# State-space groups: the gated y moves into the upper squares tiles, and GpSimd takes two steps of the group's tail

## The chip, the cores and the metric

The kernel runs on one core of one Trainium2 chip. The core has a matrix engine (TensorE; PE in the profile, its weight loads PEld), VectorE (DVE), ScalarE (ACT), GpSimd (POOL) and SyncE (SP), which here only issues DMAs. The metric is device time in microseconds of one execution. The kernel before took 1147.05 us, the median of 3 runs from 1146.51 to 1148.46.

## The reference

A sequence of 256 tokens of width 1024 goes through three layers in float32: sparse attention with a convolved feed-forward layer, retention with another, and a hybrid layer. The change lies in the hybrid layer's state-space branch:

```python
y = ssd_chunked_scan(x32 * dt[..., None], dt * a_cont, bmat, cmat)
y = y + d_skip.astype(jnp.float32)[:, None] * x32
y = y.reshape(b, seq, D_INNER).astype(h.dtype) * jax.nn.silu(z)
y = rmsnorm(y.reshape(b, seq, SSD_GROUPS, D_INNER // SSD_GROUPS),
            ssd_norm_w.reshape(SSD_GROUPS, D_INNER // SSD_GROUPS))
y_ssd = y.reshape(b, seq, D_INNER) @ w_branch_ssd
```

There are four groups of 512 channels. In each, y is gated by silu(z) and normalised over the 512 channels of its group. Beside this branch run a pooling branch and two gates; their products are merged afterwards.

## The kernel before

Every matrix product is computed in three passes of a reduced format: a weight is split into a high part (ScalarE, `split_hi`, line 235) and a low part (VectorE, `split_lo`, line 240: raw minus high), and so is each operand. Weights come as 512 KB slabs of 128 x 1024 through a ring of six; TensorE works a slab in 24 matmuls (lines 248 to 250), some 2.7 us.

In the state-space stage each engine has its own program in a fixed order, tied to the others by semaphores. A group has 12 slabs, j = 0 to 11. Slabs 0 to 5 are B, C and four tiles of x: ScalarE evicts the slab with the first tap of the convolution (line 1840), VectorE adds the three others (line 2009, which read PSUM), ScalarE applies silu (line 1789). At j = 6 TensorE turns x (`turn`, lines 1660 and 1663, which wait for the last silu). Slabs 6 to 9 are z, 10 and 11 are the pooling input. From j = 6 on the decays are made: VectorE's `gaps` (line 1991), ScalarE's exponentials (line 1805), VectorE's `weighted` (line 1997), which TensorE's `head_pair` (lines 1674 and 1676) waits for, in the four buffers `seen`.

The rest of a group, its tail, is done during the next group (that of the last group during the gate slabs m = 0 to 15 that follow). Its steps, by the slab at which they stand:

- j = 0: VectorE adds the skip (line 1952) and multiplies by silu(z) into `z_s` (line 1961).
- j = 1: ScalarE squares it into tiles 0 to 3 of `sq` (line 1771); VectorE adds the four tiles in two instructions (`add_four`, line 344), 512 and 256 columns wide.
- j = 2: after its slab TensorE sums over the partitions (`tail_sums`, line 1612), in order, so that a late sum holds up all slabs behind it.
- j = 3: ScalarE's root (line 382), three VectorE steps to the inverse (lines 387 to 389).
- j = 6: VectorE scales y (line 1970, four instructions), reading each row with a step of two and writing two contiguous halves, into `y_f`. ScalarE copies the high part into `b_hi` (line 1777).
- j = 7: VectorE computes the low part into `b_lo` (line 1976). `y_f` shares memory with two of the `seen` buffers, so `gaps(2)` waits for this step (`yssd_ready`).

GpSimd's program in this stage is one DMA per group (line 2512), which waits for the group's last gap and spreads the next group's cumulated decays to all partitions.

Of the kernel before, what the change touches and what calls it, by code (L numbers as in the profile page):

```python
# [79 lines left out]
def halves_wide(x):  # L80

    return x.rearrange("p m (a t) -> p m a t", a=2)


def woven(x):
# [53 lines left out]
def build(nc, x, stream, ada, c_rows, params, consts, out):  # L139
    ctx = ExitStack()  # L140
    with ctx:
# [1388 lines left out]
        tail = top[0]  # L1530
        x_tok2 = area(NB, 512)
        y_seen = area(4 * SEQ + 2 * SEEN)
        y_f = y_seen[:, 0:4 * SEQ].rearrange("p (a t) -> p a t", a=4)
        seen = [y_seen[:, c:c + SEEN] for c in (4 * SEQ, 4 * SEQ + SEEN, 0, SEEN)]
        cum_rows = nc.dram_tensor("cum_rows", (GROUPS, GROUP_HEADS * SEQ), F32, kind="Internal").ap()
        cum_all = c_hi.bitcast(F32)
# [225 lines left out]
        def ssd_act(act):  # L1762
# [4 lines left out]
            def tail(j, g, it):  # L1767

                if j == 1:
                    act.wait_ge(yz_ready, in_group(1, 1, g, it))  # L1770
                    act.activation(sq[:, 0:4], z_s, ACT.Square).then_inc(ysq_ready, 1)
                if j == 3:
                    row_root(act, RS_SSD + g, ysum_ready, in_group(1, 1, g, it), 5, 512, EPS_B, it)
                if j == 6:
                    act.wait_ge(yn_ready, in_group(1, 1, g, it))
                    o = slice(4 * g, 4 * g + 4) if it is None else bass.ds(it * 4 + 4 * g, 4)
                    act.activation(b_hi[:, o], y_f, ACT.Copy).then_inc(yhi_ready, 1)

            def group(g, it=None):
                def prm(t, j):  # L1780
# [117 lines left out]
            for m in range(NT):  # L1898
# [4 lines left out]
                if m == 2:  # L1903
                    act.activation(shift_hi_cols, mlp_shift, ACT.Copy).then_inc(shift_hi, 1)

        def win_of(g):

            return win[g % 2]

        def ssd_vec(dve, step):  # L1910
# [44 lines left out]
            def tail(j, g, it):  # L1955

                if j == 0:
                    skip(2, g, it)
                    skip(3, g, it)
                    dve.wait_ge(z_silu, in_group(1, 1, g, it))  # L1960
                    dve.tensor_tensor(z_s, cv[:, 2:6], z_s, ALU.mult).then_inc(yz_ready, 1)
                if j == 1:
                    dve.wait_ge(ysq_ready, in_group(1, 1, g, it))
                    add_four(dve, ADDED_SSD + 2 * g, 2, it)
                if j == 3:
                    row_inv(dve, step, RS_SSD + g, 5, 512, EPS_B, inv_s, inv_s_ready, it)
                if j == 6:
                    dve.wait_ge(inv_s_ready, in_group(1, 1, g, it))
                    for t in range(4):
                        ins = dve.scalar_tensor_tensor(out=halves(y_f[:, t]), in0=parted(z_s[:, t]), scalar=prm(34 + t, g, it), in1=parted(inv_s),  # L1970
                                                       op0=ALU.mult, op1=ALU.mult)
                    ins.then_inc(yn_ready, 1)
                if j == 7:
                    dve.wait_ge(yhi_ready, in_group(1, 1, g, it))
                    o = slice(4 * g, 4 * g + 4) if it is None else bass.ds(it * 4 + 4 * g, 4)
                    dve.tensor_tensor(b_lo[:, o], y_f, b_hi[:, o].bitcast(F32), ALU.subtract).then_inc(yssd_ready, 1)

            def group(g, it=None):
                def heads_of(c, n=1):
# [2 lines left out]
                def gaps(k):  # L1982
                    if k == 2:
                        dve.wait_ge(rows_landed, in_group(16, 16, g, it))
                    if k == 2 and g:
                        dve.wait_ge(yssd_ready, in_group(1, 1, g - 1, it))
                    if k >= 4:
                        dve.wait_ge(y_done, in_group(k - 3, 8, g, it))
                    for b in range(NB):
                        c = slice(0, SEQ) if b == 0 else slice(SEQ, SEEN)  # L1990
                        dve.tensor_scalar(seen[k % 4][:, c], cum_all[:, k, b * P:SEQ], cum_tok[:, b, heads_of(k)], 0.0,
                                          ALU.subtract, ALU.min).then_inc(gap_ready, 1)
# [4 lines left out]
                        dve.tensor_tensor(seen[k % 4], seen[k % 4], cb, ALU.mult).then_inc(seen_ready, 1)  # L1997

                for j in range(GRP):
                    if g and j != 7:  # L2000
                        tail(j, g - 1, it)
                    if j < 7 and not (g and j == 1):
                        split_lo(dve, S_GRP + GRP * g + j + (4 if g and j == 0 else 3), it, GRP)
                    if not g and j == 0:
                        steps_by_token()
                    if j < 6:
                        dve.wait_ge(tap_done, in_group(j + 1, 6, g, it))
                        for n in range(1, 4):
                            ins = dve.scalar_tensor_tensor(out=cv[:, j, n:SEQ], in0=ps[:, j % 4, 0:SEQ - n], scalar=prm(5 * j + 3 - n, g, it),  # L2009
                                                           in1=cv[:, j, n:SEQ], op0=ALU.mult, op1=ALU.add)  # L2010
                            if n < 3:
                                step(ins)
                        ins.then_inc(conv_done, 1)
                    if not g and j in (0, 2):
                        {0: softplus, 2: rows}[j]()
                    if j == 5:
                        dve.wait_ge(cb_ready, in_group(1, 1, g, it))
                        dve.scalar_tensor_tensor(out=cb, in0=const("tri", SEEN), scalar=-1.0, in1=ps[:, 4, 0:SEEN],
                                                 op0=ALU.is_gt, op1=ALU.mult).then_inc(cb_masked, 1)
                    if j == 4 and not g:  # L2020
                        dve.wait_ge(own_ready, 3)
                        dve.tensor_copy(cum_tok.rearrange("p b h -> p (b h)"), ps[:, 5, 64:128]).then_inc(own_copied, 1)
                        dve.wait_ge(own_copied, 1)
                    if j == 7:
                        dve.wait_ge(cb_masked, in_group(1, 1, g, it))
                        for b in range(NB):
                            dve.wait_ge(x_turned, in_group(b + 1, 2, g, it))
                            dve.tensor_tensor(x_tok2[:, b].rearrange("p (h d) -> p h d", h=GROUP_HEADS),
                                              ps[:, 5 + b, :].rearrange("p (h d) -> p h d", h=GROUP_HEADS),
                                              dt_tok[:, b, heads_of(0, GROUP_HEADS)].unsqueeze(2).broadcast_to((P, GROUP_HEADS, SSD_P)), ALU.mult).then_inc(x_tok_ready, 1)  # L2030
                        weighted(0)
                    if g and j == 7:
                        tail(j, g - 1, it)
                    if j > 8:
                        weighted(2 * (j - 8))
                    if j in (9, 10):
                        gaps(2 * (j - 7))
                        gaps(2 * (j - 7) + 1)
                    if j >= 7:
                        split_lo(dve, S_GRP + GRP * g + j + 3, it, GRP)  # L2040
                    if j == 7:
                        gaps(2)
                        gaps(3)
                    if j == 11:
                        skip(0, g, it)
                        skip(1, g, it)
                        split_lo(dve, S_GRP + GRP * g + j + 4, it, GRP)
# [4 lines left out]
                group(1, it)  # L2052
            step.leave(GROUPS - 1)
            dve.wait_ge(u_done, 2 * GROUPS)
            step(dve.memset(sq[:, NT - 1], 1.0))

            def pool(g):

# [2 lines left out]
                if g == GROUPS - 1:  # L2061
                    w = 2 ** (g + 1)
                    cur, running = win[g % 2], win[(g + 1) % 2]
                    for t in range(2):
                        ins = dve.tensor_tensor_scan(running[:, t], sq[:, NT - 1], u[:, t], 0.0, ALU.mult, ALU.add)
                    step(ins)
                    dve.tensor_copy(cur[:, :, 0:w], running[:, :, 0:w])
                    step(dve.tensor_tensor(cur[:, :, w:SEQ], running[:, :, w:SEQ], running[:, :, 0:SEQ - w], ALU.subtract))
# [26 lines left out]
            for m in range(2 * NT):  # L2095
                if m == GATES_FIRST:
                    pools()
                tail(m, GROUPS - 1, None)
                if m - 1 == POOL_AT[-1]:
                    pooled_lo(GROUPS - 1)  # L2100
                if m:
                    lo_ahead(dve, gate_at(m) + 3)
                if m in POOL_AT:
                    pool(POOL_AT.index(m))
                if m - 1 in POOL_AT and m - 1 != POOL_AT[-1]:
                    pooled_lo(POOL_AT.index(m - 1))
# [395 lines left out]
        def _(pool):  # L2502
# [5 lines left out]
            for g in range(GROUPS):  # L2508
                if g:
                    pool.wait_ge(first_gaps, 4 * g)  # L2510
                    pool.wait_ge(gap_ready, 12 * g)
                pool.dma_start(cum_all, cum_rows[g:g + 1].rearrange("a (h t) -> a h t", t=SEQ).broadcast_to((P, GROUP_HEADS, SEQ))).then_inc(rows_landed, 16)
            pool.wait_ge(mod_ready, 1)
            pool.dma_start(row_cols[0].rearrange("(m p) -> p m", p=P), mod[:, 5 * NT:6 * NT], allow_slow_non_contiguous=True).then_inc(rows_stored, 16)
            pool.dma_start(row_cols[1].rearrange("(m p) -> p m", p=P), pcol("final_w", n=NT), allow_slow_non_contiguous=True).then_inc(rows_stored, 16)
# [174 lines left out]
```

## Time and profile before

| | |
|---|---|
| profiled execution | 1148.47 us |
| its span (first to last instruction) | 1146.7 us |
| clock granted to TensorE, mean | 0.996 |
| state-space groups 0 to 3, from the first slab | about 687 to 833 us |
| gate slabs | about 832 to 880 us |

Times are microseconds from the span's start. In the timelines a row is: start, duration, engine, line, operation, output<-input with shapes, count, and in brackets the idle time of the engine just before with what ended it. Rows of several instructions are merged, and one starts a little before the end of the one ahead of it.

### The profile page before, as it was taken

How to read it: one execution, taken by the hardware profiler on the slowest of the kernel's cores; microseconds unless marked ns; L12 is line 12 of the kernel's file. 1: busy time of each engine (PE TensorE's matmuls, PEld its weight loads, DVE VectorE, ACT ScalarE, POOL GpSimd, SP SyncE). 2: the span in 40 equal slices, each digit the busy share in tenths (PEclk: the TensorE clock that was granted, in tenths of full speed). 3: DMA queues.
4: the chain of work that ended last, by engine and by line, in shares of the span. 5: the costliest groups of instructions: out<-in, count | busy, mean ns of one | idle time of the engine just before them, and what ended most of it. 6: DMA issues, size and time to landing. Idle time of an engine off the chain costs nothing.

```text
span 1146.7 us, 25636 instructions
## 1 busy us (share of the span) xinstructions
PE 1116.8 (97%) x9126; PEld 1076.4 (94%) x9126; DVE 978.8 (85%) x1785; ACT 711.4 (62%) x1109; POOL 34.7 (3%) x64
## 2 busy tenths in 40 slices
PE   8989999999999999999999999999999999999997
PEld 7989999999899999999999989999899999999997
DVE  7877999998998998989999889999997678766667
ACT  6557656666556556565666677878876457645554
POOL 0000000000000100000000000000000000000000
PEclk9999999999999999999999999999999999999999
DMA  8534676675566866856766537457546556665661
GB/s 289 177 119 155 210 238 233 221 262 186 192 251 258 308 225 245 302 198 238 237 209 212 183 101 255 146 202 155 186 155 232 174 197 217 214 198 199 200 202 38
DMA packets 73042, 235.73 MB, mean 206 GB/s; under 512 B 7425, under 2 KB 16641, under 8 KB 72849
## 3 DMA queue, kind: packets, MB, share of 16 engines
q1 hardware_dynamic: 64304, 203.86, 53.4%
q0 software_dynamic: 8528, 30.98, 7.9%
q8 instruction: 42, 0.69, 0.2%
q14 instruction: 24, 0.19, 0.1%
q10 hardware_dynamic: 144, 0.02, 0.0%
HBM read 233.73 MB, written 1.09 MB: 205 GB/s over the span
## 4 chain that ended last, share of the span: by engine, by line
PE 73%; DVE 17%; issue 4%; ACT 4%; DVEq 1%; DMA 1%; ACTq 0%; SPq 0%; another core or an unknown queue 0%
PE ps L248 22%; PE ps L250 21%; PE ps L249 21%; DVE w_lo L240 5%; PE ps L280 3%; PE ps L282 2%; DVE arena L2009 1%; ACT w_hi L235 1%; DVE arena L502 1%; DVE arena L939 1%; DMA w_raw<-stream 1%; DVE arena L1997 0%; PE ps L1674 0%; DVE arena L974 0%; ACT sq L421 0%
## 5 line engine op out<-in xcount | busy, mean ns | idle before, releaser
L240 DVE TENSOR_TENSOR w_lo<-w_raw,w_hi 128x1024 fp32r<-128x1024 f32 x381 | 461.1, 1218 | 11.1 <-ACT w_hi L235 5.1
L248 PE MATMUL ps<-a_hi,w_hi 128*128 128x256 f32 x1656 | 463.8, 280 | 4.8 <-DVE w_lo L240 3.2
L250 PE MATMUL ps<-a_hi,w_lo 128*128 128x256 f32 x1656 | 456.2, 276 | 0.0
L249 PE MATMUL ps<-a_lo,w_hi 128*128 128x256 f32 x1656 | 456.1, 275 | 0.0
L235 ACT ACTIVATE w_hi<-w_raw 128x1024 fp32r<-128x1024 f32 x381 | 390.7, 1049 | 20.9 <-DMA w_raw<-stream 11.8
L248 PEld LDWEIGHTS ps<-a_hi,w_hi 128*128 128x128 f32 x1656 | 318.5, 192 | 12.0 <-issue 5.5
L249 PEld LDWEIGHTS ps<-a_lo,w_hi 128*128 128x128 f32 x1656 | 318.5, 192 | 0.6 <-issue 0.2
L250 PEld LDWEIGHTS ps<-a_hi,w_lo 128*128 128x128 f32 x1656 | 318.7, 192 | 0.0
L248 PE MATMUL ps<-b_both,w_hi 128*128 128x256 f32 x560 | 155.7, 278 | 2.2 <-DVE b_both L999 1.3
L249 PE MATMUL ps<-b_both,w_hi 128*128 128x256 f32 x560 | 154.0, 275 | 0.0
L250 PE MATMUL ps<-b_both,w_lo 128*128 128x256 f32 x560 | 154.0, 275 | 0.0
L248 PEld LDWEIGHTS ps<-b_both,w_hi 128*128 128x128 f32 x560 | 107.4, 192 | 4.9 <-DVE b_both L999 2.6
L250 PEld LDWEIGHTS ps<-b_both,w_lo 128*128 128x128 f32 x560 | 107.5, 192 | 0.0
L249 PEld LDWEIGHTS ps<-b_both,w_hi 128*128 128x128 f32 x560 | 107.5, 192 | 0.0
L1098 ACT ACTIVATE arena<-arena,par 128x256 f32<-128x256 f32 x88 | 52.5, 599 | 57.3 <-DVE arena L1159 57.3
L248 PE MATMUL ps<-c_both,w_hi 128*128 128x258 f32 (+1 forms) x280 | 77.2, 276 | 0.8 <-DVE w_lo L240 0.8
L249 PE MATMUL ps<-c_both,w_hi 128*128 128x258 f32 (+1 forms) x280 | 77.0, 275 | 0.0
L250 PE MATMUL ps<-c_both,w_lo 128*128 128x258 f32 (+1 forms) x280 | 77.0, 275 | 0.0
L1109 ACT ACTIVATE b_both<-arena 128x256 fp32r<-128x256 f32 x44 | 18.4, 418 | 73.3 <-DVE arena L1173 73.3
L502 DVE CUSTOM_DVE_ANT_0 arena<-arena 128x1024 f32<-128x1024 f32 x48 | 58.5, 1218 | 1.6 <-DMA arena<-ada 1.6
L2268 ACT ACTIVATE arena<-arena 128x256 f32<-128x256 f32 x32 | 16.3, 510 | 65.4 <-DVE arena L2333 65.4
L248 PEld LDWEIGHTS ps<-c_both,w_hi 128*128 128x128 f32 x280 | 53.5, 191 | 1.0 <-issue 1.0
(315 smaller groups left out, 1683.1 us busy)
## 6 DMA issues: line engine op xcount, KB each, us to landing
w_raw<-stream SPq DMA_DIRECT2D x381, 512.0 KB, 4.2
arena<-ada POOLq DMA_DIRECT2D x48, 512.0 KB, 5.9
c_both<-cum_rows POOLq DMA_DIRECT2D x4, 1024.0 KB, 8.7
arena<-x SPq DMA_DIRECT2D x2, 512.0 KB, 4.5
con<-consts SPq DMA_DIRECT2D x1, 1024.0 KB, 5.7
arena<-row_cols POOLq DMA_DIRECT2D x2, 512.0 KB, 5.2
arena<-c_rows POOLq DMA_DIRECT2D x1, 512.0 KB, 4.2
out<-arena SPq DMA_DIRECT2D x2, 256.0 KB, 2.2
```

The source lines that it names most:

```text
L235: act.activation(w_hi[:, s % RING], w_raw[:, s % RING], ACT.Copy).then_inc(w_hi_ready, 1)
L240: dve.tensor_tensor(w_lo[:, s % RING], w_raw[:, s % RING], w_hi[:, s % RING].bitcast(F32), ALU.subtract).then_inc(w_lo_ready, 1)
L248: pe.matmul(o, wh, xh, start=start, stop=False, skip_group_check=shared)
L249: pe.matmul(o, wh, xl, start=False, stop=False, skip_group_check=shared)
L250: return pe.matmul(o, wl, xh, start=False, stop=stop, skip_group_check=shared)
L280: pe.matmul(ps[:, bank, :].rearrange("p (i t a) -> p i t a", i=2, a=2), w_hi[:, s % RING, t], both[:, k].rearrange("p i (a t) -> p i t a", ...
L282: mm = pe.matmul(by_two(ps[:, bank, 0:SEQ]), w_lo[:, s % RING, t], woven(both[:, k, 0]), start=False, stop=last and k == NT - 1)
L502: dve.tensor_tensor_reduce(ada_raw[:, DOT_BUF[i]], ada_raw[:, DOT_BUF[i]], cond_row, 1.0, 0.0, ALU.mult, ALU.add, o).then_inc(dot_done, 1)
L939: ins = dve.scalar_tensor_tensor(out=score[:, q_part[b]], in0=rel[:, n % 2, i * w:(i + 1) * w], scalar=w_idx[:, b, h:h + 1], in1=const("ad ...
L1098: act.activation(conv[:, p % 2, half], up[:, p % 2, half], ACT.Identity, bias=prm(p, 6 + half, it), scale=prm(p, 3 * half + 2, it)).then_i ...
L1109: act.activation(b_hi[:, p % 4], glu[:, p % 2], ACT.Copy).then_inc(f["hi"], 1)
L2268: act.activation(relu[:, n % 3], up_m[:, n % 3], ACT.Relu, bias=up_shift[:, n % 3:n % 3 + 1]).then_inc(relu_ready, 1)
```

## The change

The gated y is written into tiles 4 to 7 of `sq` in place of `z_s`, squared from there, and scaled in place by contiguous rows, so that it no longer shares memory with the `seen` buffers. The step of two moves to the readers: ScalarE's high part and the low part read y with a step of two and write contiguous halves. `add_four` and the low part go from VectorE's program to GpSimd's, behind the DMA of the group that is running; the last group's are behind the last DMA and ahead of two small DMAs (lines 2514 and 2515). VectorE no longer waits for the low part at j = 7, but at j = 11, ahead of the next skip. The tile of ones for the pooling scan moves from `sq` tile 7 to tile 3, and its memset from the end of the groups to gate slab m = 5.

```diff
+def parted_four(x):
+
+    return x.rearrange("p m (t a) -> p m a t", a=2)
...
-        y_f = y_seen[:, 0:4 * SEQ].rearrange("p (a t) -> p a t", a=4)
+        y_f = sq[:, 4:8]
...
-                    act.activation(sq[:, 0:4], z_s, ACT.Square).then_inc(ysq_ready, 1)
+                    act.activation(sq[:, 0:4], y_f, ACT.Square).then_inc(ysq_ready, 1)
...
-                    act.activation(b_hi[:, o], y_f, ACT.Copy).then_inc(yhi_ready, 1)
+                    act.activation(halves_wide(b_hi[:, o]), parted_four(y_f), ACT.Copy).then_inc(yhi_ready, 1)
...
+        def ssd_pool(pool, g):
+
+            pool.wait_ge(ysq_ready, g + 1)
+            add_four(pool, ADDED_SSD + 2 * g, 2, None)
+            pool.wait_ge(yhi_ready, g + 1)
+            y, hi, lo = parted_four(y_f), halves_wide(b_hi[:, 4 * g:4 * g + 4]), halves_wide(b_lo[:, 4 * g:4 * g + 4])
+            pool.tensor_tensor(lo, y, hi.bitcast(F32), ALU.subtract).then_inc(yssd_ready, 1)
...
-                    dve.tensor_tensor(z_s, cv[:, 2:6], z_s, ALU.mult).then_inc(yz_ready, 1)
-                if j == 1:
-                    dve.wait_ge(ysq_ready, in_group(1, 1, g, it))
-                    add_four(dve, ADDED_SSD + 2 * g, 2, it)
+                    dve.tensor_tensor(y_f, cv[:, 2:6], z_s, ALU.mult).then_inc(yz_ready, 1)
...
-                        ins = dve.scalar_tensor_tensor(out=halves(y_f[:, t]), in0=parted(z_s[:, t]), scalar=prm(34 + t, g, it), in1=parted(inv_s),
+                        ins = dve.scalar_tensor_tensor(out=y_f[:, t], in0=y_f[:, t], scalar=prm(34 + t, g, it), in1=inv_s,
                                                        op0=ALU.mult, op1=ALU.mult)
                     ins.then_inc(yn_ready, 1)
-                if j == 7:
-                    dve.wait_ge(yhi_ready, in_group(1, 1, g, it))
-                    o = slice(4 * g, 4 * g + 4) if it is None else bass.ds(it * 4 + 4 * g, 4)
-                    dve.tensor_tensor(b_lo[:, o], y_f, b_hi[:, o].bitcast(F32), ALU.subtract).then_inc(yssd_ready, 1)
...
-                    if k == 2 and g:
-                        dve.wait_ge(yssd_ready, in_group(1, 1, g - 1, it))
...
+                    if g and j == 11:
+                        dve.wait_ge(yssd_ready, in_group(1, 1, g - 1, it))
...
-            step(dve.memset(sq[:, NT - 1], 1.0))
...
+                if m == 5:
+                    step(dve.memset(sq[:, 3], 1.0))
...
                 pool.dma_start(cum_all, cum_rows[g:g + 1].rearrange("a (h t) -> a h t", t=SEQ).broadcast_to((P, GROUP_HEADS, SEQ))).then_inc(rows_landed, 16)
+                if g:
+                    ssd_pool(pool, g - 1)
+            ssd_pool(pool, GROUPS - 1)
```

## Rows read from the trace of the kernel before

**Rows 1.** Busy time by stretch: us, then each engine's busy time, clock, DMA share.
```profile
690.00:734.00 44.00, 43.40 (x382) 41.61 (x382) 40.16 (x73) 34.42 (x57) 0.89 (x1) 0.99 0.62 215
734.00:774.50 40.50, 38.14 (x337) 36.28 (x336) 38.11 (x69) 32.56 (x52) 0.88 (x1) 1.00 0.53 182
835.00:870.00 35.00, 32.77 (x290) 32.40 (x289) 31.53 (x58) 23.69 (x35) 0.00 (x0) 1.00 0.45 150
870.00:893.00 23.00, 23.00 (x179) 22.23 (x179) 14.44 (x14) 14.46 (x24) 0.00 (x0) 1.00 0.73 252
```

**Rows 2.** Who waited for whom, 690 to 870 us: total, times, longest.
```profile
PE ps L1663 <- ACT arena L1789: 3.8, 3, 1.6
PE ps L1674 <- DVE arena L1997: 2.3, 3, 0.8
PE ps L248 <- DVE w_lo L240: 2.2, 2, 1.4
```

**Rows 3.** Timeline of TensorE: its stops, and the sums of two tails.
```profile
732.97 0.44 PE L1663 MATMUL ps<-con,arena 128*128 128x128 f32 x2 [0.60 <-ACT arena L1789]
743.21 0.65 PE L1674 MATMUL ps<-arena 128*64 128x256 f32 x4 [0.77 <-DVE arena L1997]
759.16 0.60 PE L1612 MATMUL ps<-sq,con 128*128 128x256 f32 x2
773.38 0.44 PE L1663 MATMUL ps<-con,arena 128*128 128x128 f32 x2 [1.59 <-ACT arena L1789]
...
860.72 0.35 PE L248 MATMUL ps<-a_hi,w_hi 128*128 128x256 f32 x1 [1.38 <-DVE w_lo L240]
869.84 0.35 PE L248 MATMUL ps<-c_both,w_hi 128*128 128x256 f32 x1 [0.85 <-DVE w_lo L240]
```

**Rows 4.** Timeline of VectorE around the squares' adds, during group 2's first slabs.
```profile
757.71 1.14 DVE L344 TENSOR_TENSOR sq<-sq 128x512 f32<-128x512 f32 x2
758.77 1.73 DVE L2009 SCALAR_TENSOR_TENSOR arena<-ps,par,arena 128x255 f32<-128x255 f32 x3
```

**Rows 5.** Timeline of VectorE around the low part, same group.
```profile
773.25 1.78 DVE L1970 SCALAR_TENSOR_TENSOR arena<-arena,par 128x256 f32<-128x256 f32 x4
...
778.22 1.22 DVE L1976 TENSOR_TENSOR b_both<-arena,b_both 128x1024 f32 x1
779.35 1.22 DVE L240 TENSOR_TENSOR w_lo<-w_raw,w_hi 128x1024 fp32r<-128x1024 f32 x1
780.49 1.00 DVE L1991 TENSOR_SCALAR arena<-c_both,arena 128x256 f32<-128x256 f32 x4
```

**Rows 6.** Timeline of VectorE in the last group's tail, at the gate slabs.
```profile
837.15 1.15 DVE L344 TENSOR_TENSOR sq<-sq 128x512 f32<-128x512 f32 x2 [1.12 <-ACT sq L1771]
...
843.84 0.42 DVE L387 SCALAR_TENSOR_TENSOR diag<-diag 128x256 f32<-128x256 f32 x1 [0.70 <-ACT diag L382]
```

**Rows 7.** Groups of VectorE instructions, 690 to 870 us: busy us, mean ns.
```profile
L1970 DVE SCALAR_TENSOR_TENSOR arena<-arena,par 128x256 f32<-128x256 f32 x16 | 7.2, 512 | 0.0
L389 DVE SCALAR_TENSOR_TENSOR arena<-diag 128x256 f32<-128x256 f32 x4 | 1.7, 424 | 0.1
```

**Rows 8.** Timeline of ScalarE: the squares, a decay's exponential, the high part.
```profile
755.04 1.06 ACT L1771 ACTIVATE sq<-arena 128x1024 f32<-128x1024 f32 x1 [0.27 <-DVE arena L1961]
776.86 1.04 ACT L1777 ACTIVATE b_both<-arena 128x1024 f32 x1
781.07 0.99 ACT L1805 ACTIVATE arena<-arena 128x384 f32<-128x384 f32 x2 [0.73 <-DVE arena L1991]
```

**Rows 9.** Timeline of GpSimd: one group's DMA, as in each of the three later groups.
```profile
747.60 0.88 POOL L2512 DMA_DIRECT2D c_both<-cum_rows  x1 [40.11 <-DVE arena L1991]
```

**Rows 10.** Groups of instructions of the whole span: GpSimd's, and ScalarE's copy by two.
```profile
L863 POOL TENSOR_TENSOR rs_root<-rs_var,minus_half 128x6 f32<-128x6 f32 x1 | 1.4, 1362 | 67.7 <-DVE rs_var L950 67.7
L2518 POOL DMA_DIRECT2D arena<-row_cols x1 | 0.6, 566 | 178.6 <-DVE res L2147 178.6
...
L1878 ACT ACTIVATE c_both<-arena 128x512 fp32r<-128x512 f32 x4 | 3.1, 787 | 5.1 <-DVE arena L2078 5.1
```

More of the change, by code:

```diff
@@ L1999, in group @@
                 for j in range(GRP):
-                    if g and j != 7:
+                    if g:
                         tail(j, g - 1, it)
@@ L2031, in group @@
                         weighted(0)
-                    if g and j == 7:
-                        tail(j, g - 1, it)
                     if j > 8:
@@ L2064, in pool @@
                     for t in range(2):
-                        ins = dve.tensor_tensor_scan(running[:, t], sq[:, NT - 1], u[:, t], 0.0, ALU.mult, ALU.add)
+                        ins = dve.tensor_tensor_scan(running[:, t], sq[:, 3], u[:, t], 0.0, ALU.mult, ALU.add)
                     step(ins)
@@ L2512, in _ @@
                 pool.dma_start(cum_all, cum_rows[g:g + 1].rearrange("a (h t) -> a h t", t=SEQ).broadcast_to((P, GROUP_HEADS, SEQ))).then_inc(rows_landed, 16)
+                if g:
+                    ssd_pool(pool, g - 1)
+            ssd_pool(pool, GROUPS - 1)
             pool.wait_ge(mod_ready, 1)
```

## The prediction

> **What bounds the kernel now.** I read the busy time by stretch first. In the period of one group, 734 to 774.5 us, TensorE is busy for 38.14 of 40.50 us and VectorE for 38.11 [rows 1]. The two are level, neither has room, and who waits for whom has to be read from the waits. From 690 to 870 us TensorE waited 3.8 us for the last silu at the turn of x, 2.3 us for a decay at the second head pair, 2.2 us for a weight's low part [rows 2]. Its timeline places them: in this period 0.77 and 1.59, which is the whole 2.36 that the stretch lacks; at the gate slabs 1.38 and 0.85 [rows 3]. All of them end with VectorE: the silu follows its convolution steps, the decay is its own product, the low part its subtraction. After 870 us TensorE is busy for 23.00 of 23.00 us [rows 1], so what is won before 870 arrives at the end, and nothing is won later.
>
> What can be won is bounded there. The turn in group 1 waits 0.60 us [rows 3], before VectorE has fallen behind; I take 0.60 as what stays of each of the three. That leaves 3.8 - 3 x 0.6 = 2.0 at the turns, 2.3 at the head pairs and 2.2 at the gate slabs: 6.5 us at most.
>
> **The change part by part.**
>
> *The squares' adds leave VectorE.* From 757.71 to the next instruction at 758.77 they take 1.06 us [rows 4], four times: 4.2 us. In the last tail VectorE also waited 1.12 us for the squares [rows 6]; that goes as well.
>
> *The low part leaves VectorE.* From 778.22 to 779.35 is 1.13 us [rows 5], four times: 4.5 us. It stands just ahead of a weight split and of the gaps on which the second head pair depends, so here the 0.77 us hang on it directly.
>
> *The scaling becomes contiguous.* It takes a mean of 512 ns by steps of two, and a contiguous instruction of the same kind and width 424 [rows 7]: 0.09 us x 4 x 4 = 1.4 us.
>
> *The memset* only changes its place: nothing.
>
> Together VectorE loses 4.2 + 1.1 + 4.5 + 1.4 = 11.2 us of work and waiting. Not all of it counts: at 843.84 it waited 0.70 us for ScalarE's root [rows 6], which hangs on TensorE's sum and comes no sooner because VectorE does. I take another 0.7 off: 10.5 us.
>
> *ScalarE's high part now reads by steps of two.* A 512-wide copy of that kind took 787 ns, a 1024-wide contiguous one 1.04 us, a contiguous 384-wide exponential 0.5 (two in 0.99) [rows 8, 10]. The contiguous 512 lies near 0.62, so twice the excess is 0.3 us. Soon after it ScalarE idles 0.73 us for the gaps [rows 8], which hides it; without that cover it is 0.3 x 4 = 1.3 us.
>
> *GpSimd's queue.* The adds and the low part stand behind the DMA of the running group, issued at 747.60 after a wait of 40.11 us [rows 9]; the squares end at 755.04 + 1.06 = 756.10 [rows 8], so the queue is free. Its low part must end before the next DMA, 40 us later, and does. The two DMAs now behind the last low part feed one that waited 178.6 us for something else [rows 10]. These moves cost nothing.
>
> *What GpSimd's instructions take.* The only two-operand instruction there took 1.36 us for six columns, a power [rows 10]. VectorE's own times are the lower bound, and those plus 1.36 for each instruction the upper: adds 1.06 to 3.8 us, low part 1.2 to 2.6 us.
>
> The Trainium skill, "GPSIMD Engine Reference" (3.1), gives 4497 ns for a float32 add of 2048 columns; by that, as an estimate, the adds take 1.7 and the low part 2.25 us, inside both bounds. No row here shows it.
>
> The adds have from 756.10 to TensorE's sum at 759.16 [rows 3, 8]: 3.06 us. Up to there they are free. VectorE meanwhile runs convolution steps, one operand of which lies in PSUM [rows 4].
>
> The low part falls among instructions of VectorE with two operands in SBUF, or from SBUF to SBUF: weight splits, gaps, products [rows 5]. No row shows VectorE beside a GpSimd elementwise instruction. The bounds for how long one such step holds VectorE up, h, are 0, if the two don't disturb each other, and its whole 2.6 us. I take the middle of the bounds for its own duration, (1.2 + 2.6) / 2 = 1.9 us, since some of its 1.36 us of start-up need not occupy memory. The cost is 4 x 1.9 = 7.6 us.
>
> *The new wait at j = 11* stands ahead of the skip, with the convolutions of the next group behind it. The low part starts about 778 us and the wait comes some ten later: nothing.
>
> **The sum.** The gain is the smaller of 6.5 and 10.5 - 4h: with h = 1.9 it is 2.9, rounded to 3.0 us. The profiled execution took 1148.47 us, 1.4 over the median of 1147.05, with the same span to lose from; I take the 3.0 off the median: **1144.0 us**.
>
> **The rivals.**
>
> *VectorE is held up for the whole low part.* With h = 2.6 the gain is 10.5 - 10.4, next to nothing: **1146.9 us**. For it speaks that both engines work on SBUF alone at that point; against it that nothing in this trace shows such a hold.
>
> The Trainium skill's page "SBUF — State Buffer" (Who interferes with whom) states this rule: an instruction of VectorE with two SBUF inputs contends with a GpSimd one that reads SBUF, and the later of the two waits for the whole of the other. It is a rule against this change, and why this rival gets a fourth of the chance. With the other page's 2.25 us, as an estimate, the sum would be 1.5 us of gain.
>
> *They don't disturb each other.* Then h is below (10.5 - 6.5) / 4 = 1.0, and TensorE's 6.5 us bound: **1140.5 us**. For it speaks that VectorE's stops on TensorE are so short; against it the shared data and time.
>
> *The adds come too late, and it gets slower.* The place is `tail_sums`, ahead of all slabs. From 3.06 us on each us of the adds costs TensorE four; from 3.06 + 6.5 / 4 = 4.7 us on, more than all other stops are worth. The upper bound of 3.8 stays below. If each add also waits for one split of VectorE (1.22, [rows 5]), it is 6.2: (6.2 - 3.06) x 4 - 6.5 = +6.1, **1153 us**; half way from 4.7 it is 1150. Against it: the neighbours there are convolution steps.
>
> *It doesn't relieve VectorE*: the wait at j = 11 gives the time back. 1147 us.
>
> **How the numbers follow.** Forecast 0.40 (own range 1142.3 to 1145.8), whole hold 0.24, undisturbed 0.22, late adds 0.09, no relief 0.05. A measurement tells 0.2%, 2.3 us, from no change. Faster by more: three quarters of the forecast (0.30), the undisturbed case (0.22), a little of the whole hold (0.03): 0.55. Slower: the late adds, 0.09. Within: 0.36. The range is 1140.0 to 1148.5: it takes in the undisturbed case and h up to nearly 3, and leaves out most of the late adds.
>
> **What would show it.** Right: no add or low part on VectorE, its scaling near 0.42 us; the stop at the second head pair shorter or as it was, the turns nearer 0.6, the stops at 860 and 870 shorter; one VectorE instruction longer, or a gap before it, beside each low part of GpSimd, by some 1.9 us. Wrong: GpSimd's adds over 3 us with a stop of TensorE at line 1612; no trace of a hold, with the stops gone (1140.5); or a hold as long as the low part.

## The result, and the profile after

The changed kernel takes 1150.24 us, the median of 10 runs from 1149.41 to 1151.93; the kernel before, on the same chip, 1147.18 us (10 runs, 1146.51 to 1148.46). The ratio is 1.0026 with an interval from 1.0018 to 1.0034: slower by 3.1 us. Forecast were 1144.0 and at most 1148.5. The profiled execution took 1150.93 us and its span 1149.1, 2.4 more than the span before. In both profiled executions the clock granted to TensorE is well below full speed in the same two stretches of 5 us, means of time at 2.4 and at 1.2 GHz: 0.66 in both from 65 to 70 us, 0.70 before and 0.69 after from 685 to 690 (ahead of them TensorE had been busy for 2.8 and 2.9, and for 4.4 and 4.2, of 5 us). So their difference is not one of clock.

Lines have moved by some numbers: the turn is now 1668, the second head pair 1679, the gaps 1995, `weighted` 2001, the scaling 1980, the high part 1782, a weight's low part 245, a slab's matmuls 253 to 255, and GpSimd's adds and low part are 349 and 1917.

First, as in [rows 1], the busy time by stretch (us, then busy PE, PEld, DVE, ACT, POOL, clock, DMA share, GB/s):

```profile
733.28:773.73 40.45, 38.05 (x335) 36.19 (x336) 37.98 (x66) 32.61 (x51) 6.23 (x4) 1.00 0.52 183
...
864.00:866.00 2.00, 2.00 (x21) 2.00 (x20) 2.00 (x4) 1.54 (x3) 0.00 (x0) 1.00 0.06 10
866.00:868.00 2.00, 2.00 (x20) 2.00 (x19) 1.90 (x7) 0.00 (x0) 0.00 (x0) 1.00 0.28 43
868.00:870.00 2.00, 2.00 (x20) 2.00 (x19) 1.08 (x3) 1.56 (x2) 0.00 (x0) 1.00 0.20 23
...
870.00:893.00 23.00, 21.71 (x172) 20.81 (x171) 15.17 (x14) 15.40 (x25) 0.00 (x0) 1.00 0.79 277
```

GpSimd now works 6.23 us in a group, and VectorE is as busy as before: 37.98 us where it was 38.11. Three instructions (two adds and the low part) have left it and its busy time has hardly fallen, so others must have become longer. The group is no shorter either: 40.45 us from turn to turn (773.63 - 733.18 below), before 40.41 (773.38 - 732.97, [rows 3]).

Who waited for whom, 690 to 872 us, against [rows 2]:

```profile
PE ps L1679 <- DVE arena L2001: 5.0, 3, 1.7
PE ps L253 <- DVE w_lo L245: 2.7, 2, 1.9
PE ps L1668 <- ACT arena L1794: 2.4, 3, 0.9
```

The wait for a decay at the second head pair has gone from 2.3 to 5.0 us and is now the largest; the one at the turn has gone from 3.8 to 2.4. TensorE's timeline places them, against [rows 3]:

```profile
733.18 0.44 PE L1668 MATMUL ps<-con,arena 128*128 128x128 f32 x2 [0.95 <-ACT arena L1794]
744.35 0.65 PE L1679 MATMUL ps<-arena 128*64 128x256 f32 x4 [1.69 <-DVE arena L2001]
773.63 0.44 PE L1668 MATMUL ps<-con,arena 128*128 128x128 f32 x2 [0.71 <-ACT arena L1794]
...
862.46 0.35 PE L253 MATMUL ps<-a_hi,w_hi 128*128 128x256 f32 x1 [1.92 <-DVE w_lo L245]
871.53 0.35 PE L253 MATMUL ps<-c_both,w_hi 128*128 128x256 f32 x1 [0.80 <-DVE w_lo L245]
882.98 0.35 PE L253 MATMUL ps<-a_hi,w_hi 128*128 128x256 f32 x1 [0.49 <-DVE w_lo L245]
```

With the rows left out (the third turn 0.72, the other two head pairs 1.68 each) the whole 2.4 us can be added up:

| stops of TensorE, us | before | after | |
|---|---|---|---|
| first turn shown | 0.60 | 0.95 | +0.35 |
| the two turns after it | 1.59 + 1.59 | 0.71 + 0.72 | -1.75 |
| second head pair, three groups | 0.77 x 3 | 1.69 + 1.68 + 1.68 | +2.74 |
| gate slabs | 1.38 + 0.85 | 1.92 + 0.80 | +0.49 |
| from the restart after these to the end | 1146.7 - 869.84 | 1149.1 - 871.53 | +0.71 |
| ahead of the first turn | | | -0.14 |
| sum | | | +2.40 |

Four lines have lost. What lengthens the first turn no row here shows; for the other three the rows give a candidate, which the experiments then test. VectorE beside the low part, as in [rows 5], and in the last tail, as in [rows 6]:

```profile
778.36 1.21 DVE L245 TENSOR_TENSOR w_lo<-w_raw,w_hi 128x1024 fp32r<-128x1024 f32 x1
779.50 3.17 DVE L1995 TENSOR_SCALAR arena<-c_both,arena 128x256 f32<-128x256 f32 x4
...
838.67 1.23 DVE L2079 TENSOR_TENSOR arena<-arena,con 128x16 f32<-128x16 f32 x2
839.93 1.20 DVE L2081 SCALAR_TENSOR_TENSOR arena<-arena 128x512 f32<-128x512 f32 x1
...
856.37 2.28 DVE L2075 COPY arena<-arena 128x4 f32<-128x4 f32 x1
```

GpSimd at the same times:

```profile
757.32 2.09 POOL L349 TENSOR_TENSOR sq<-sq 128x512 f32<-128x512 f32 x2 [7.68 <-ACT sq L1776]
778.54 3.32 POOL L1917 TENSOR_TENSOR b_both<-sq,b_both 128x1024 fp32r<-128x1024 f32 x1 [19.13 <-ACT b_both L1782]
...
838.02 2.57 POOL L349 TENSOR_TENSOR sq<-sq 128x512 f32<-128x512 f32 x2 [15.71 <-ACT sq L1776]
856.08 2.56 POOL L1917 TENSOR_TENSOR b_both<-sq,b_both 128x1024 fp32r<-128x1024 f32 x1 [15.49 <-ACT b_both L1782]
858.58 0.91 POOL L2522 DMA_DIRECT2D row_cols<-mod  x1
859.48 0.88 POOL L2523 DMA_DIRECT2D row_cols<-par  x1
```

Read the two together. The weight split of 778.36 had begun before the low part, and ends on time; the low part takes 3.32 us here and 2.56 at 856.08, so it was the one that waited. The four gaps that begin at 779.50 take 3.17 us for 1.00 in [rows 5] and end at 782.67, 0.81 us after the low part (781.86): VectorE was held for 2.17 us. In the last tail a copy of four columns takes 2.28 us, and ends at 858.65, as the low part beside it does (858.64).

ScalarE, against [rows 8], and where it waits for the weight stream (the left number in brackets):

```profile
777.12 1.35 ACT L1782 ACTIVATE b_both<-sq 128x1024 f32 x1
...
873.27 1.06 ACT L240 ACTIVATE w_hi<-w_raw 128x1024 fp32r<-128x1024 f32 x1 [2.83 <-DMA w_raw<-stream]
```

Last, VectorE's scaling by lines, 690 to 870 us (busy us, mean ns), against [rows 7]: 478 ns, where 424 was expected.

```profile
L1980 DVE SCALAR_TENSOR_TENSOR sq<-sq,par,arena 128x256 f32<-128x256 f32 x16 | 6.7, 478 | 0.0
```

### The profile page after: what moved, and what is told of

The parts are those of the page before. It is cut to its first block, busy times and chain, and to the rows that moved or that the text cites. A ratio compares the mean times of both kernels' runs of the same rounds, so it can differ in the third digit from the quotient of the medians.

```text
span 1149.1 us, 25627 instructions
## 1 busy us (share of the span) xinstructions
PE 1118.3 (97%) x9126; PEld 1077.7 (94%) x9126; DVE 978.5 (85%) x1773; ACT 712.1 (62%) x1109; POOL 55.7 (5%) x76
## 4 chain that ended last, share of the span: by engine, by line
PE 73%; DVE 16%; issue 5%; ACT 4%; DMA 1%; DVEq 1%; SPq 0%; ACTq 0%
PE ps L253 21%; PE ps L255 21%; PE ps L254 21%; DVE w_lo L245 5%; PE ps L285 3%; PE ps L287 2%; DMA w_raw<-stream 1%; DVE arena L507 1%; ACT w_hi L240 1%; DVE arena L2013 1%; DVE arena L1415 1%; PE ps L1679 1%; DVE arena L944 1%; DVE arena L1459 1%; DVE arena L979 0%
```

## The experiments

The ratios are to the kernel before on the same chip, with a 95% interval. The code is shortened to the lines and arguments that matter. The theory: VectorE is held for the whole of a GpSimd instruction, and the hold lies where the second head pair waits. Its rivals: the high part, now strided, is late; the hold has nothing to do with shared access to SBUF; its length counts and not its place.

### One part of the change at a time

`adds_only` puts the low part back on VectorE at j = 7:

```diff
 ssd_pool:
-    pool.tensor_tensor(lo, y, hi.bitcast(F32), ALU.subtract).then_inc(yssd_ready, 1)
 ...
 VectorE's tail:
+    if j == 7: dve.tensor_tensor(<the same>)
```

> The low part goes back to VectorE at its old place (j = 7); GpSimd keeps the squares' adds, y stays in sq. Theory A (the low part on GpSimd holds VectorE's first gap instruction for about 2.2 us, right ahead of the second head pair, and that is the whole loss): GpSimd's adds stay 2.1 us and free, the head pair's stop returns to about 0.8 us, the turns stay near 0.7; 1143.5 to 1146 us, faster than before by 1 to 3.5. Theory B (the adds on GpSimd cost, by a later root and by holds of VectorE at the gate slabs): as slow as the changed kernel, 1149 to 1150.5. Theory C (reading y by steps of two, on ScalarE above all, costs): 1149 to 1150.5 too.

`lo_only` puts the adds back instead:

```diff
 ssd_pool:
-    add_four(pool, ADDED_SSD + 2 * g, 2, None)
 ...
 VectorE's tail:
+    if j == 1: add_four(dve, ADDED_SSD + 2 * g, 2, it)
```

> The squares' adds go back to VectorE at j = 1; GpSimd keeps the low part. Theory A: the hold of 2.2 us stays and the relief at j = 1 is gone, so the turns wait longer again: 1150 to 1152.5 us. Theory B: the loss goes, 1146 to 1147.5. Theory C: unchanged, 1149.5 to 1151.

`layout_only` does both, so that only y's place and the order of its columns are changed:

```diff
-            ssd_pool(pool, GROUPS - 1)
 ...
 VectorE's tail:
+    if j == 1: add_four(dve, ...)
+    if j == 7: dve.tensor_tensor(<the low part>)
```

> Adds and low part both on VectorE at their old places; only the place and order of y in memory are those of the change. Theory A and B: the steps of two move from the scaling to the high and the low part and cost or give nothing beyond 0.15 us per group, 1146.5 to 1148 us, the same as before. Theory C: 1149 to 1150.5.

Measured: adds_only 0.9990 [0.9981, 0.9999], lo_only 1.0038 [1.0025, 1.0052], layout_only 1.0011 [1.0002, 1.0020]. TensorE's stops in group 2, first adds_only, then lo_only, then layout_only:

```profile
772.05 0.44 PE L1668 MATMUL ps<-con,arena 128*128 128x128 f32 x2 [0.72 <-ACT arena L1794]
782.67 0.65 PE L1679 MATMUL ps<-arena 128*64 128x256 f32 x4 [1.15 <-DVE arena L2002]
```

```profile
773.93 0.44 PE L1668 MATMUL ps<-con,arena 128*128 128x128 f32 x2 [1.59 <-ACT arena L1794]
785.09 0.65 PE L1679 MATMUL ps<-arena 128*64 128x256 f32 x4 [1.68 <-DVE arena L2002]
```

```profile
773.54 0.44 PE L1668 MATMUL ps<-con,arena 128*128 128x128 f32 x2 [1.61 <-ACT arena L1794]
784.15 0.65 PE L1679 MATMUL ps<-arena 128*64 128x256 f32 x4 [1.14 <-DVE arena L2000]
```

The two moves act at different places, and in these stops they add up. The adds on GpSimd shorten the turn (1.61 to 0.72) and leave the head pair's stop as it was; the low part on GpSimd lengthens the head pair's stop (1.14 to 1.68) and leaves the turn. The third share lies in the layout alone, 0.77 to 1.14: the high part, by steps of two, takes 1.37 us there for 1.04, and VectorE's low part, 1.33 us for 1.22, waits 0.32 us for it:

```profile
778.67 1.33 DVE L1981 TENSOR_TENSOR b_both<-sq,b_both 128x1024 f32 x1 [0.32 <-ACT b_both L1782]
```

So the rival of the late high part is partly right, where VectorE computes the low part.

### Is it the shared access to SBUF?

`gaps_two_inputs` computes the gaps of decays 2 and 3 by an instruction with a second input in SBUF (zeros, with the minimum):

```diff
-    dve.tensor_scalar(seen, cum_all, cum_tok, 0.0, subtract, min)
+    dve.scalar_tensor_tensor(seen, in0=cum_all, scalar=cum_tok, in1=zero, subtract, min)
```

> The changed kernel with the gaps of decays 2 and 3 as scalar_tensor_tensor with a second SBUF input (one column of zeros, repeated) in place of tensor_scalar. Theory H1 (GpSimd's two-operand instruction shuts out every VectorE instruction that needs a second SBUF input as well as the fast tensor_scalar): the first gap is held as before, near 2.5 us, time as the changed kernel, ratio to before 1.002 to 1.004. Theory H2 (only the fast single-input instructions are shut out): no gap over 0.6 us, head pair's stop near 0.5 us, ratio 0.997 to 0.999.

`gaps_psum` has the second input in PSUM instead; it computes zeros, so it leaves out these two decays of each group:

```diff
+    dve.scalar_tensor_tensor(seen, in0=cum_all, scalar=3e38, in1=ps[:, 4, ...], is_gt, mult)
```

> The changed kernel with the gaps of decays 2 and 3 as scalar_tensor_tensor whose second input lies in PSUM; they compute zeros, so these two decays of each group are left out. H1: the gaps are not held, and the weight split behind them is held for the rest of GpSimd's instruction, 0.7 to 1.2 us; the head pair's stop falls to about 0.8 us, ratio to before 0.999 to 1.001. H2: nothing is held, ratio 0.997 to 0.999.

Measured: 1.0043 [1.0028, 1.0059] and 0.9996 [0.9986, 1.0005]. VectorE in group 2, gaps_two_inputs and then gaps_psum:

```profile
779.74 3.57 DVE L1997 SCALAR_TENSOR_TENSOR arena<-c_both,arena,con 128x256 f32<-128x256 f32 x4
```

```profile
778.91 1.14 DVE L1996 SCALAR_TENSOR_TENSOR arena<-c_both,ps 128x256 f32<-128x256 f32 x4
779.97 2.40 DVE L245 TENSOR_TENSOR w_lo<-w_raw,w_hi 128x1024 fp32r<-128x1024 f32 x1
```

The head pair's stop in the two, in the same order:

```profile
785.43 0.65 PE L1679 MATMUL ps<-arena 128*64 128x256 f32 x4 [2.08 <-DVE arena L2006]
783.35 0.65 PE L1679 MATMUL ps<-arena 128*64 128x256 f32 x4 [0.83 <-DVE arena L2005]
```

With PSUM the same four gaps run in 1.14 us beside the low part, and the hold passes to the next weight split: 2.40 us instead of 1.22, which ends with the low part. The head pair's stop falls from 1.68 in the changed kernel to 0.83; with both inputs in SBUF it grows to 2.08. This decides for the shared access: held were instructions of VectorE with two inputs in SBUF (these gaps, the split), and the gaps' own form, which has one; the same instruction with its second input in PSUM was not. The Trainium skill, "SBUF — State Buffer" (Who interferes with whom), says both: two inputs in SBUF contend with a GpSimd instruction that reads it, `tensor_scalar` and copies can do so in their fast mode, and the one that starts first keeps the ports to its end. The traces agree, in both directions (the low part's 3.32 us instead of 2.56).

### Does the length of the hold decide, or its place?

`pool_lo_after_gaps` leaves the low part on GpSimd and issues it behind the group's last gap, in front of the next adds; VectorE waits for it at the next gating product instead of at j = 11:

```diff
             if g:
-                ssd_pool(pool, g - 1)
+                if g > 1: ssd_low(pool, g - 2)
+                ssd_adds(pool, g - 1)
 ...
```

> The changed kernel with GpSimd's low part behind the last gap of the running group (behind its DMA), and VectorE's wait for it moved to the next gating product. No fast tensor_scalar follows there, only weight splits, products and skips. H1: a weight split or a product of decays is held by 1.5 to 2.3 us near the third head pair, the second head pair's stop goes to 0.5 us; ratio to before 0.998 to 1.002. H2: no instruction is held, ratio 0.996 to 0.998.

Measured: 0.9979 [0.9970, 0.9988], 1144.97 us. TensorE's waits from 690 to 876 us (with the turn of group 0, 0.61 us), then GpSimd, then VectorE in that kernel:

```profile
PE ps L1668 <- ACT arena L1794: 3.6, 4, 1.2
PE ps L253 <- DVE w_lo L245: 2.8, 2, 1.9
```

```profile
745.38 4.04 POOL L1920 TENSOR_TENSOR b_both<-sq,b_both 128x1024 fp32r<-128x1024 f32 x1
```

```profile
745.92 1.22 DVE L245 TENSOR_TENSOR w_lo<-w_raw,w_hi 128x1024 fp32r<-128x1024 f32 x1
747.05 1.10 DVE L1968 SCALAR_TENSOR_TENSOR arena<-arena,par,ps 128x256 f32<-128x256 f32 x2
748.27 2.23 DVE L245 TENSOR_TENSOR w_lo<-w_raw,w_hi 128x1024 fp32r<-128x1024 f32 x1
```

The low part takes longer than in the changed kernel, 4.04 us (5.42 behind the last group's gaps), and still holds a split by 1.0 us. But the stop at the second head pair is gone altogether, for 0.5 us more at each of the last two turns (1.18 instead of 0.72). The same work on the same engine goes from 1.0026 to 0.9979 by where it is issued. This run does not separate length from place, for the hold is shorter too, 1.0 us for 2.17: the split of 745.92 ran first, and the two steps of 747.05, which read PSUM, ran on beside the low part.

`no_low` leaves the low part out, to see what remains without its hold:

```diff
-            pool.tensor_tensor(lo, y, hi.bitcast(F32), ALU.subtract).then_inc(yssd_ready, 1)
+            pool.sem_inc(yssd_ready, 1)
```

> The changed kernel without any low part of y (it is left out; the operand keeps what lay there). This is the changed kernel with a hold of nothing. If relief of VectorE adds up wherever it falls, as the prediction's sum had it (the smaller of 6.5 and 10.5 us), the ratio to before is 0.994 to 0.995. If a group is worth what its own two stops lose (turn 1.59 to 0.72, second head pair 0.77 to what the strided high part leaves, some 0.3), it is some 1.3 us in each of two groups and 0.5 in the first, and 1 to 2 at the gate slabs: ratio 0.9955 to 0.9975.

Measured: 0.9962 [0.9947, 0.9976], a gain of 4.4 us (0.0038 x 1148). With the adds on GpSimd and no low part anywhere, the head pairs no longer stop, but the turns still stop 0.96, 0.72 and 0.72 us, and the gate slabs 0.78 and 0.51:

```profile
770.00 0.44 PE L1668 MATMUL ps<-con,arena 128*128 128x128 f32 x2 [0.72 <-ACT arena L1794]
873.74 0.35 PE L253 MATMUL ps<-a_hi,w_hi 128*128 128x256 f32 x1 [0.51 <-DVE w_lo L245]
```

### VectorE's low part one slab later

`lo_later` is adds_only with the low part at j = 8, behind the gaps that the second head pair needs; `order_at_gate` also puts the columns in order in the gating product (1.33 us there), so that the high and low parts are contiguous:

```diff
 lo_later:
+    if j == 8: dve.tensor_tensor(<the low part>)
 ...
 order_at_gate, besides:
-    dve.tensor_tensor(y_f, cv[:, 2:6], z_s, ALU.mult)
+    dve.tensor_tensor(halves_wide(y_f), parted_four(cv[:, 2:6]), parted_four(z_s), ALU.mult)
```

> As the kernel with only the adds on GpSimd, but VectorE computes the low part one slab later (j = 8), behind the gaps that the second head pair needs; y no longer shares memory with the decays, so it may. Theory A: the 0.8 us stop at the second head pair goes too (three times), 1141 to 1144 us, the fastest of the four. Theories B and C: 1149 to 1150.5.

> Adds on GpSimd, low part on VectorE at j = 8, and the reordering of the tokens moved to the gating product at j = 0 (reads by steps of two, writes halves), so that square, sum, inverse, scaling, high and low part are all contiguous. Theory A2 (the strided high part, 1.37 instead of 1.04 us on ScalarE ahead of the exponentials, is what lengthens the second head pair's stop by 0.37 us): that stop falls from 0.7 to about 0.35 us, 0.1 us more at the gating; 1 to 2 us faster than the kernel with the low part at j = 8, ratio to before 0.9965 to 0.998. Rival (the strided high part is hidden, and the head pair's stop there has another cause): ratio 0.998 to 0.999, the stop unchanged.

Measured: 0.9983 [0.9974, 0.9992] and 0.9974 [0.9965, 0.9984]. The head pair's stop in the first, then the second:

```profile
782.51 0.65 PE L1679 MATMUL ps<-arena 128*64 128x256 f32 x4 [0.71 <-DVE arena L2002]
```

```profile
781.56 0.65 PE L1679 MATMUL ps<-arena 128*64 128x256 f32 x4 [0.65 <-DVE arena L2002]
```

One slab later takes the stop from 1.15 to 0.71, with the low part on VectorE as in adds_only: here the step is the same and only its place differs (and with it the wait for the high part), so the place counts. The contiguous order was to bring the stop to 0.35 and brought it to 0.65: with the low part out of the way the high part's 0.33 us are not what the head pair waits for. Between the two ratios the intervals overlap.

### The last tail, and the best of both

`gate_last_late` is order_at_gate with the last group's low part at gate slab 10 instead of 8; `both_moves` joins it with pool_lo_after_gaps (GpSimd does the first three low parts, behind the gaps, and VectorE the last; the two small DMAs then follow GpSimd's last adds, at 835 us):

```diff
 gate_last_late:
-    if j == 8:
+    if j == (10 if g == GROUPS - 1 else 8):
```

> As the kernel with the order made at the gating product, low part on VectorE; only the last group's low part moves from gate slab 8 to gate slab 10, where VectorE idles 0.9 us for ScalarE, and ScalarE's wait for it moves from slab 8 to the pooling products. If that idle time takes it: the two stops at the gate slabs, 0.2 and 1.5 us, fall to 1.0 together, ratio to before 0.9965 to 0.998. If the chain there ends at ScalarE or TensorE: no difference to 0.9974.

> GpSimd keeps the adds and the low parts of the first three groups, these behind each group's last gap; the order is made at the gating product; the last low part is VectorE's at gate slab 10. If place decides, not the length of the hold: no stop at the second head pair, turns at 0.6 to 1.2 us, gate stops near 1 us together; ratio to before 0.995 to 0.997, the fastest of all. Rival (a hold costs VectorE wherever it falls): no faster than the kernel with all low parts on VectorE, 0.997 to 0.998.

Measured: 0.9980 [0.9964, 0.9997] and 0.9963 [0.9950, 0.9975], that is 1142.67 us against 1148.03 of the kernel before in that comparison. TensorE's waits of both_moves, 690 to 876 us:

```profile
PE ps L1668 <- ACT arena L1794: 3.1, 3, 1.2
PE ps L253 <- DVE w_lo L245: 1.1, 1, 1.1
```

gate_last_late cuts the stops at the gate slabs to 1.06 us, from 1.67 in order_at_gate (0.19 and 1.48), but its ratio can't be told from that one's. both_moves beats both kernels of this case: no stop at the head pairs, 1.05 us at the gate slabs. It does all the work and is as fast as no_low.

### The two small DMAs

In the ledger 0.71 us lie behind the stage, and there the stream moved 10 to 43 GB/s. `rows_first` puts the two DMAs back ahead of GpSimd's last tail:

```diff
-            ssd_pool(pool, GROUPS - 1)
             pool.wait_ge(mod_ready, 1)
             pool.dma_start(row_cols[0]..., mod[:, 5 * NT:6 * NT])
             pool.dma_start(row_cols[1]..., pcol("final_w", n=NT))
+            ssd_pool(pool, GROUPS - 1)
```

> The changed kernel with only the two small DMAs (the row of gates and of final weights) put ahead of GpSimd's last adds and low part, where the kernel before has them in time (788 instead of 858 us). Theory E (these DMAs, beside the weight stream at 858 to 868 us, hold it up, and the pooling stage pays): ScalarE no longer waits 2.8 us for a weight of the stream near 873 us, the stream moves over 150 GB/s from 864 to 870 us instead of 10 to 43, and from TensorE's restart at the pooling products to the end of the span it is 276.9 us instead of 277.6; the kernel's ratio to the one before is 1.0020 instead of 1.0026, that is 1149.5 us; the stops at the turns, at the second head pair and at the gate slabs stay 0.7, 1.68 and 1.9. Rival: the stream's pause comes from somewhere else (the last low part itself, or the order of the weights): the stretch stays 277.6 us and the ratio 1.0026.

Measured: 1.0021 [1.0012, 1.0030]. Its busy time by stretch (columns as above):

```profile
825.00:830.00 5.00, 5.00 (x31) 4.68 (x32) 5.00 (x13) 3.84 (x7) 0.00 (x0) 0.66 0.36 26
...
864.00:866.00 2.00, 2.00 (x20) 2.00 (x20) 1.97 (x3) 2.00 (x5) 0.00 (x0) 1.00 0.46 156
868.00:870.00 2.00, 2.00 (x21) 2.00 (x20) 1.64 (x5) 0.26 (x1) 0.00 (x0) 1.00 0.83 328
```

TensorE's restart there:

```profile
872.89 0.35 PE L253 MATMUL ps<-c_both,w_hi 128*128 128x256 f32 x1 [0.84 <-DVE w_lo L245]
```

From there to the end it is 1149.7 - 872.89 = 276.8 us instead of 277.6, and the wait for the stream and the stop of 0.49 us are gone: the trace decides for E. The other runs agree. Six kernels issue the two DMAs between 849 and 861 us, the changed one among them, and in each ScalarE waits 2.8 to 3.0 us for the stream; in the other eight it doesn't. From the restart to the end it is 277.5 to 277.7 us in the four of the six that have this restart, and 276.8 to 276.9 in the eight. no_low is one of the four, so the last low part is not the cause. The stream's slow stretch has gone along with the DMAs, to 825 us, where nobody waits for it. The total doesn't decide: 1.0020 was expected, and the interval holds 1.0026 too. One thing went against the expectation: the head pair beside the DMAs stopped 2.01 us, not 1.68, and behind it the clock granted to TensorE was 0.66 on the mean from 825 to 830 us, between its levels of 1.2 and 2.4 GHz. Whether the DMAs caused the 0.33 us wasn't separated.

## Why the prediction was wrong

*What bounds the kernel* was right for the stage: all its stops end with VectorE, and what it lost is found again at the end. That nothing changes behind it was not: 0.71 us were lost there.

*The squares' adds* were right. They take 2.09 us of the 3.06 that they had, TensorE's sum never waited, and the convolution steps beside them, which read PSUM, weren't held. The rival of late adds is out. The relief of 1.06 us shortened a turn by 0.87. It did so twice. At the first turn VectorE had not fallen behind, and the stop there grew by 0.35, as in every kernel with the adds on GpSimd except the two with the low part behind the gaps; what does that wasn't tested.

*The low part's price* came out near, in part by luck. h was put at 1.9 between 0 and 2.6, and is 2.17 us at the gaps. But 1.9 was the middle of two bounds for the low part's own duration, which is 2.5 to 2.6 us, and the start-up for which it allowed is not there (last section). The rival of the whole hold had the mechanism, and its 1146.9 us came out of the same sum, so it missed as well.

*The step that failed is the sum*: "The gain is the smaller of 6.5 and 10.5 - 4h". With the measured h it gives 10.5 - 8.7 = 1.8 us of gain, and so 1145.3 us; measured are 3.1 us of loss. It treats VectorE's time as one purse, in which what is freed at j = 1 pays for what is held at j = 7. TensorE stops in between, at the turn, and waits until VectorE has caught up: relief ahead of it is paid out there, 0.87 us at most, and none is left for the head pair (1.14 us in layout_only, 1.15 in adds_only). So each place has to be summed by itself. At the head pair the low part's 1.13 us went [rows 5] and 2.17 came: +1.04, where the stop grew by 0.91. The prediction had both numbers, "so here the 0.77 us hang on it directly" and h = 1.9; taken there alone they say 3 x (1.9 - 1.13) = 2.3 us of loss, and the row shows 2.7. That the stop falls to 0.83 in gaps_psum and vanishes in pool_lo_after_gaps, with the low part still on GpSimd, shows that it is the hold at this place.

*The strided high part* was to hide in ScalarE's idle time. Its excess is right (0.31 us, forecast 0.3), its cover is not: with the low part on VectorE the layout adds 0.37 us to the stop, and VectorE waits 0.32 us for the high part (layout_only). What it adds in the changed kernel was not separated.

*"These moves cost nothing"* failed for the two small DMAs. The prediction looked at who waits for their data, and not at the transfers beside them: some 0.7 us, by rows_first and the runs beside it.

*The last tail* was expected to gain: 1.06 + 1.12 + 1.13 us of relief. VectorE was held for 0.97 us at 838.67 and 0.5 at 839.93 (the same steps take 0.26 and 0.69 later in this trace), and for 2.1 at 856.37, and TensorE's stops there grew by 0.49. The first of them, 1.38 us before and 1.92 after, is 1.07 with the low part back on VectorE (adds_only) and gone without it (no_low), so the growth goes with the last low part on GpSimd.

*The scaling* was mis-sized: 34 ns less instead of 88, that is 0.5 us instead of 1.4.

*The undisturbed case* (1140.5) was bounded too low as well: no_low, with no hold at all, gains 4.4 us and not 6.5, since the turns keep 0.72 to 0.96 us each instead of 0.60, and the gate slabs 0.78 and 0.51 instead of nothing.

## What to carry to other kernels

Where two engines meet at several points in each period, relief ends at the next point at which one waits for the other: sum gains and costs by the stop at which they arrive, never over the period. Before elementwise work goes to GpSimd, list which VectorE instructions stand beside it: in these traces those with an operand in PSUM ran on, and splits, gaps and copies from SBUF to SBUF were held to its end. With the low part issued behind the gaps the kernel went from a loss of 0.26% to a gain of 0.21%. A DMA that nobody waits for can still cost, through the stream that it runs beside.

## What the runs showed of the hardware

- The 1.36 us of [rows 10] for six columns is no start-up of other GpSimd instructions: the adds took 1.40 us for 512 columns and 0.74 for 256 (means, 690 to 870 us), the low part 2.5 to 2.6 for 1024 where it had little to wait for.
- Two DMAs of 4 KB each, in single elements from GpSimd's queue, went with a stream at 10 to 43 GB/s for some 6 us. The slow stretch followed them in rows_first. The Trainium skill, "DMA: Bandwidth & Descriptors" (Rules for kernel authors), says that a strided last dimension is cut into one descriptor per element. What of the 6 us comes from that no run here separates.
- A copy of four columns on VectorE, 0.17 us by itself, took 2.28 beside a GpSimd instruction: here the hold went by what was left of GpSimd's instruction, not by the size of what was held.
